# Seven slots for gathered rows where there were eight, three weight units kept and two parked, longer rows in two loads

## What is computed

```python
h = rmsnorm(x, norm_mix)
u_s5, x_lru, y_lru, g_a, g_b = split(h @ w_in)
a_out = s5_branch(u_s5, ...)          # diagonal complex scan, gelu, GLU (w_glu)
b_out = rglru_branch(x_lru, y_lru, ...)
merged = sigmoid(g_a) * (a_out @ w_proj_a) + sigmoid(g_b) * (b_out @ w_proj_b)
x = x + merged @ w_out
q = (rmsnorm(x, norm_ffn) @ w_q).reshape(C, 8, 2, 128)
s = einsum('chsk,hsnk->chsn', q, sub_keys)      # two top-16 lists, then top 16 of their sums
act = gelu(einsum('chkd,cd->chk', u_tab[eidx], x))
x = x + einsum('chk,chkd->cd', softmax(cs) * act, v_tab[eidx])
y = rmsnorm(x, norm_final)
```

## Time and profile before

| | before |
|---|---|
| median of three runs | 3239.21 us |
| the profiled execution | 3233.47 us, its span 3231.3 us |
| PE busy | 2726.6 us, 84% |
| DVE busy | 2491.7 us, 77% |
| ACT busy | 975.0 us, 30% |
| POOL busy | 1230.0 us, 38% |
| moved by DMA | 1245.43 MB, mean 385 GB/s |
| first gather | at 249.4 us |

### The profile page before, as it was taken

The page is one execution under the profiler, slowest core; times in us unless marked ns, Lnnn a source line. Parts: engine busy times, 40 slices in busy tenths (PEclk is TensorE's granted clock), DMA queues, the critical chain, the costliest instruction groups (busy, mean ns, idle before and its releaser), DMA issues.

```text
span 3231.3 us, 31776 instructions
## 1 busy us (share of the span) xinstructions
PE 2726.6 (84%) x9312; PEld 1564.3 (48%) x9312; DVE 2491.7 (77%) x5858; ACT 975.0 (30%) x3001; POOL 1230.0 (38%) x1048
## 2 busy tenths in 40 slices
PE   7988988999878989898879989899989895666566
PEld 6774544666444546555435545566534452222122
DVE  6836888888678898887669888887678887666754
ACT  2112433232134342322134432322133442222223
POOL 0003444344343443343344443333344343545553
PEclk9999999999989999999989999999999998787789
DMA  4269999999999999999999999999999998999997
GB/s 137 89 214 384 406 420 416 412 387 409 418 415 376 407 420 415 385 420 418 418 418 389 419 420 406 413 393 381 417 409 419 419 412 316 421 408 422 421 421 329
DMA packets 207197, 1245.43 MB, mean 385 GB/s; under 512 B 28056, under 2 KB 36632, under 8 KB 74928
## 3 DMA queue, kind: packets, MB, share of 16 engines
q0 software_dynamic: 148608, 1082.20, 81.6%
q1 hardware_dynamic: 56912, 156.36, 13.0%
q10 hardware_dynamic: 1504, 4.85, 0.4%
HBM read 1238.76 MB, written 4.55 MB: 385 GB/s over the span
## 4 chain that ended last, share of the span: by engine, by line
DMA 39%; PE 27%; DVE 23%; issue 3%; ACT 3%; DVEq 3%; POOL 2%; ACTq 1%; POOLq 0%
DMA arena<-in_uv,arena 39%; PE psum L1770 14%; DVE arena L1420 10%; PE psum L1671 7%; DVE arena L1020 4%; DVE arena L1012 3%; ACT arena L697 2%; PE psum L1815 2%; POOL arena L656 2%; PE psum L1686 1%; PE psum L1806 1%; PE psum L1827 1%; DVE arena L1261 1%; PE psum L1656 1%; PE psum L1706 1%
## 5 line engine op out<-in xcount | busy, mean ns | idle before, releaser
L656 POOL DMA_INDIRECT arena<-in_uv,arena x1032 | 1226.0, 1188 | 1973.8 <-PE psum L1770 1366.3
L1770 PE MATMUL psum<-arena 128*128 128x512 f32 x3192 | 1604.2, 647 | 434.8 <-ACT arena L697 400.5
L1420 DVE CUSTOM_DVE_ANT_0 arena<-arena 128x1024 f32<-128x1024 f32 x1024 | 1235.8, 1224 | 509.2 <-DMA arena<-in_uv,arena 478.2
L1770 PEld LDWEIGHTS psum<-arena 128*128 128x128 f32 x3192 | 621.6, 203 | 1264.7 <-issue 611.1
L697 ACT ACTIVATE arena<-arena 128x128 f32<-128x128 f32 (+3 forms) x2481 | 697.9, 313 | 1599.1 <-DVE arena L1420 1453.1
L1671 PE MATMUL psum<-arena 128*128 128x256 f32 (+1 forms) x2688 | 623.4, 387 | 12.3 <-DVE arena L1020 6.4
L1671 PEld LDWEIGHTS psum<-arena 128*128 128x128 f32 x2688 | 517.4, 194 | 142.9 <-issue 72.3
L1020 DVE SCALAR_TENSOR_TENSOR arena<-arena 128x1024 f32<-128x1024 f32 (+6 forms) x461 | 372.4, 814 | 64.3 <-ACT arena L697 34.2
L1012 DVE TENSOR_TENSOR arena<-arena 128x256 f32<-128x256 f32 (+10 forms) x832 | 284.9, 382 | 24.0 <-issue 1.6
L697 ACT ACTIVATE arena<-psum 128x256 f32<-128x256 f32 (+7 forms) x266 | 107.3, 414 | 574.9 <-PE psum L1671 506.4
L697 ACT ACT_TABLE_LOAD x113 | 145.0, 1283 | 4.0 <-PEq L2082 0.8
(11 more groups left out here) (99 smaller groups left out, 1020.8 us busy)
## 6 DMA issues: line engine op xcount, KB each, us to landing
arena<-in_w_in SPq DMA_DIRECT2D x112, 512.0 KB, 7.8
arena<-in_w_q SPq DMA_DIRECT2D x68, 512.0 KB, 11.2
arena<-in_w_ab SPq DMA_DIRECT2D x40, 512.0 KB, 7.8
arena<-in_w_out SPq DMA_DIRECT2D x40, 512.0 KB, 7.8
arena<-in_uv,arena POOLq DMA_INDIRECT x1032, 12.5
arena<-in_w_glu SPq DMA_DIRECT2D x16, 256.0 KB, 7.2
arena<-in_x_tok SPq DMA_DIRECT2D x8, 512.0 KB
arena<-in_keys SPq DMA_DIRECT2D x32, 128.0 KB, 7.4
```

What stands on the lines that cost most here:

```text
L656: pool.indirect_dma_start(uvring[:, r], None, i_["uv"], bass.IndirectOffsetOnAxis(column, 0)).then_inc(uv_in[r], 16)
L1420: V.tensor_tensor_reduce(out=u, in0=u, in1=hn[i // (SLOT // 2)], scale=1.0, scalar=0.0, op0=ALU.mult, op1=ALU.add, accum_out=dots_[:, b % ...
L1770: ins = mm(PV[:, half], dg[:, PAIR * (b % 2) + k], uvring[:, i % UV, at:at + 512], start=(i % (SLOT // 2) == 0), stop=(pe_slots(c, i + 1) ...
```

## The change

- `UV` goes from 8 to 7. The place of a gather in the ring is now its running number modulo 7 over the whole program, with the sample's eight gathers in the count (`place`, `sample_place`), and each gather waits for the one seven places before.
- `homes`: units `w_out` 2, `w_ab` 2 and `w_ab` 5 (`RESIDENT`) are loaded once in the program into places of their own; `w_out` 0 and 1 (`PARKED`) lie in `acc[1]` and `hn[1]` through chunk 0. Such a unit has no slot in the ring, and SP issues its one load without a wait. The ring counts only the others (`RINGED`, `ring_at`).
- `xT` is laid out on the host chunk by chunk, so that the load has one row of 8 KB (8.25 KB in the last chunk) in each partition.
- Keys come for two heads at once, 2 KB a partition, and lie in `gy`; before the first pair of a chunk SP waits for the end of the mix.
- To make room, `rstd` lies in `rT`, `ones` is one column read 128 times, `ztmp` lies in scratch, `pre` is gone, and `hS` is `s0`: the decay of the sample's states stands in `sample_states` behind the scans, in front of the GLU.

```diff
-UV = 8
+UV = 7
...
+RESIDENT = (("w_out", 2), ("w_ab", 2), ("w_ab", 5),)
+PARKED = (("w_out", 0), ("w_out", 1))
+HOMES = RESIDENT + PARKED
...
+def home(c, l):
+
+    kept = RESIDENT if c else HOMES
+    return HOMES.index(weight(c, l)) if weight(c, l) in kept else None
...
+RINGED = [[l for l in range(SLOTS if c else SLOTS0) if home(c, l) is None] for c in range(CH)]
...
+def place(c, i):
+
+    return SLOT * c + i + (HEADS if c == CH - 1 and i >= SA else 0)
...
+def sample_place(h):
+
+    return SLOT * (CH - 1) + SA + h
...
+        homes = [R.take(D) for _ in RESIDENT] + [acc[1], hn[1]]
...
             def load_weights(c, l):
 
-                g = slots(c) + l
-                w = weights[l] if c else weights0[l]
-                sp.dma_start(ring[:, g % RING, 0:w.shape[1]], w).then_inc(slot_in[g % RING], 16)
+                name, m = weight(c, l)
+                w = i_[name][m]
+                k = home(c, l)
+                if k is None:
+                    g = ring_at(c, l)
+                    sp.dma_start(ring[:, g % RING, 0:w.shape[1]], w).then_inc(slot_in[g % RING], 16)
+                elif c == 0 and WEIGHTS0.index((name, m)) == l:
+                    sp.dma_start(homes[k], w).then_inc(home_in[k], 16)
 
             def slot_free(c, l):
 
-                if l < RING:
-                    before, at = c - 1, (SLOTS if c > 1 else SLOTS0) - RING + l
-                else:
-                    before, at = c, l - RING
-                sp.wait_ge(unit, units(before) + slot_unit(at) + 1)
+                if home(c, l) is None:
+                    at = RINGED[c].index(l) - RING
+                    before = c if at >= 0 else c - 1
+                    sp.wait_ge(unit, units(before) + slot_unit(RINGED[before][at]) + 1)
...
-                sp.dma_start(hT[:, :, 0:n], i_["xT"][:, :, (c + 1) * C:(c + 1) * C + n]).then_inc(x_in, 16)
-
-            def keys(h, scores):
+                sp.dma_start(hT_all[:, 0:n], i_["xT"][:, at:at + n]).then_inc(x_in, 16)
+
+            def keys(pair, scores):
 
                 need(sp, s_mm, scores)
-                sp.dma_start(kb[:, h % 2], i_["keys"][:, 2 * h:2 * h + 2, :]).then_inc(key_in[h % 2], 16)
+                at = 4 * (pair % QT)
+                sp.dma_start(kb[:, pair % 2], i_["keys"][:, at:at + 4, :]).then_inc(key_in[pair % 2], 16)
...
-                    if l >= 48 and l % 2 == 0:
-                        h = (l - 48) // 2
-                        keys(h, lists(c) + h - 1)
+                    if l >= 48 and l % 4 == 0:
+                        pair = (l - 48) // 4
+                        if pair == 0:
+                            sp.wait_ge(unit, units(c) + U_OUT)
+                        keys(pair, lists(c) + 2 * (pair - 1))
...
-            def wait_free(c, i):
-
-                if on_dve(SLOT * c + i - UV):
-                    pool.wait_ge(v_dve, dve_slots(c, i - UV) + 1)
-                elif SLOT * c + i >= UV:
-                    pool.wait_ge(v_pe, pe_slots(c, i - UV) + 1)
+            def gather_to(at, column):
+
+                before = at - UV
+                if sample_place(0) <= before < sample_place(HEADS):
+                    pool.wait_ge(vs_pe, before - sample_place(0) + 1)
+                elif before >= 0:
+                    i = before - (HEADS if before >= sample_place(HEADS) else 0)
+                    if on_dve(i):
+                        pool.wait_ge(v_dve, dve_slots(0, i) + 1)
+                    else:
+                        pool.wait_ge(v_pe, pe_slots(0, i) + 1)
+                gather(at % UV, column)
...
             def slot(c, l):
-                g = slots(c) + l
+                k = home(c, l)
+                if k is not None:
+                    pe.wait_ge(home_in[k], 16)
+                    return homes[k]
+                g = ring_at(c, l)
                 pe.wait_ge(slot_in[g % RING], 16 * (g // RING + 1))
                 return ring[:, g % RING, :]
```

More of the change, by code:

```diff
@@ L67, with weight, ring_at @@
 SECOND_AT = 10
+TRUNK_W = [("w_in", m) for m in range(28)] + [("w_glu", m) for m in range(4)]
+MIX_W, OUT_W, QUERY_W = [[(name, m) for m in range(n)] for name, n in (("w_ab", 8), ("w_out", 8), ("w_q", 16))]
+WEIGHTS0 = TRUNK_W + MIX_W + OUT_W + MIX_W[0:4] + QUERY_W[0:2] + MIX_W[4:6] + QUERY_W[2:4] + MIX_W[6:8] + OUT_W \
+    + QUERY_W[4:16] + QUERY_W[0:4]
+WEIGHTS = TRUNK_W + MIX_W + OUT_W + QUERY_W
+RESIDENT = (("w_out", 2), ("w_ab", 2), ("w_ab", 5),)
+PARKED = (("w_out", 0), ("w_out", 1))
+HOMES = RESIDENT + PARKED
+def weight(c, l):
+    return WEIGHTS[l] if c else WEIGHTS0[l]
+def home(c, l):
+    kept = RESIDENT if c else HOMES
+    return HOMES.index(weight(c, l)) if weight(c, l) in kept else None
+RINGED = [[l for l in range(SLOTS if c else SLOTS0) if home(c, l) is None] for c in range(CH)]
+def ring_at(c, l):
+    return sum(len(RINGED[k]) for k in range(c)) + RINGED[c].index(l)
 TRUNK_DVE = "SSSSCSCSCSCSSSSSSS" + "LS" * 8 + "SS"
@@ L309, in build @@
         s0 = T.take(2, SJ, NS)
-        hT = T.take(KT, N)
+        hT_all = T.take(KT * N)
+        hT = [hT_all[:, 0:KT * columns(c)].rearrange("p (a b) -> p a b", a=KT) for c in range(CH)]
         ga = T.take(KT, N)
@@ L342, in build @@
         a_re, a_im = T.take(SJ), T.take(SJ)
[L343 to L344 removed]
+        hS = s0
         carr = T.take(2, SJ)
@@ L374, in build @@
         W = Arena(arena, T.at)
+        ztmp = W.take(QT, 6)
         braw = W.take(2, SJ, 16)
@@ L439, in build @@
         slot_in = [sem(f"slot_in{k}") for k in range(RING)]
+        home_in = [sem(f"home_in{k}") for k in range(len(HOMES))]
         key_in = [sem(f"key_in{k}") for k in range(2)]
@@ L574, in first_chunk @@
                     if l == 64:
-                        keys(2, 0)
-                        keys(3, 0)
+                        sp.wait_ge(unit, U_MIX1[KT - 1] + 1)
+                        keys(1, 0)
                     if l == 72:
                         next_columns(0)
-                    if l >= 72 and l % 2 == 0:
-                        h = (l - 64) // 2
-                        keys(h % HEADS, h - 1)
+                    if l >= 72 and l % 4 == 0:
+                        pair = (l - 64) // 4
+                        keys(pair, 2 * (pair - 1) if pair > 2 else 0)
                     slot_free(0, l)
@@ L674, in gathers @@
                         pool.wait_ge(s_mm, 2)
-                    wait_free(c, i)
-                    gather(i % UV, flat(idxn)[:, i:i + 1])
+                    gather_to(place(c, i), flat(idxn)[:, i:i + 1])
             for c in range(CH - 1):
@@ L684, in _ @@
             for h in range(HEADS):
[L685 to L691, removed]
+                gather_to(sample_place(h), iS[:, h:h + 1])
+            gathers(c, SA, SLOT)
         @block.scalar
@@ L1206, in c_tables, with sample_states, sample_conv @@
                 dve.sem_inc(s5_ok, 1)
[L1208 to L1216, removed]
+            def sample_states(c):
+                w = [flat(v)[:, 128 * k:128 * k + 128].rearrange("p (a b) -> p a b", b=NS) for v in (rc, rs) for k in range(2)]
+                dve.wait_ge(y_mm, SJ // 2 * (c + 1))
+                dve.wait_ge(smp_mm, 4)
+                for k, (a, x) in enumerate(((a_re, 0), (a_im, 1), (a_im, 0), (a_re, 1))):
+                    tt(w[k], over(a, NS), s0[:, x], ALU.mult)
+                dve.drain()
+                tt(s0[:, 0], w[0], w[1], ALU.subtract)
+                tt(s0[:, 1], w[2], w[3], ALU.add)
+                dve.drain()
+                tt(flat(hS.rearrange("p a b c -> p (a b) c")), flat(s0.rearrange("p a b c -> p (a b) c")),
+                   SB[0][:, 0:2 * SJ * NS], ALU.add)
+            def sample_conv():
                 for q in range(QT):
@@ L1416, in dots @@
                     i = PAIR * b + k
-                    again = 1 if c == CH - 1 and i >= SA else 0
-                    dve.wait_ge(uv_in[i % UV], 16 * (SLOT // UV * c + i // UV + 1 + again))
-                    u = uvring[:, i % UV, 0:D]
+                    at = place(c, i)
+                    dve.wait_ge(uv_in[at % UV], 16 * (at // UV + 1))
+                    u = uvring[:, at % UV, 0:D]
                     V.tensor_tensor_reduce(out=u, in0=u, in1=hn[i // (SLOT // 2)], scale=1.0, scalar=0.0, op0=ALU.mult,
@@ L1516, in first_lists @@
                 for m in range(5):
-                    mix(m, U_MIX1[m], late, MIXB[m % 2])
+                    mix(0, m, U_MIX1[m], late, MIXB[m % 2])
                 dve.wait_ge(s_ev, 1)
@@ L1593, in chunk @@
                     upto(at_mix(m) + 1)
-                    mix(m, units(c) + U_MIX + m, slice(0, n), MIXB[m % 2])
+                    mix(c, m, units(c) + U_MIX + m, slice(0, n), MIXB[m % 2])
                 upto(AT_X2)
```

77 lines of the change are left out of this document (35 added, 42 removed).

## The result

The changed kernel takes 3268.94 us (median of four runs, 3261.66 to 3273.88) where the kernel before takes 3239.03 (3235.65 to 3244.64): a ratio of 1.0092, 95% interval 1.008 to 1.0104. It is 30 us slower. The profiled execution has a span of 3271.8 us, 40.5 more than the one of before (3231.3): it is the slowest of its four, that of before the fastest. "Idle DMA time" of a stretch is its length times one less its DMA share.

What follows compares the result with a forecast made beforehand. The prediction took the DMA engines to set the pace after a start without gathers. A slot cost of 22.6 us less a gain of 17.8 gave +4.8 us, a median of 3244.0 us, range 3222 to 3272.

Steps and rivals of the forecast that it cites:

- rival 2: Stalls at nearly every trunk unit cost 52 us: +34, 3273 us; sign: idle DMA time up over 40 us; chance 0.21.
- The gain: Fewer weight loads, a shorter start and longer rows save 17.8 us in all, bounds 11.2 and 23.
- 12.0 + 2.0 + 1.0: us saved: nine loads in chunks 1 to 3, three w_out loads before the first gather, no w_out ring wait at start.
- 0.3 + 2.5: us saved: the first xT load at the start, then longer rows for later xT and key loads.
- The slot's cost: Seven slots instead of eight lose 22.6 us, where PE's trunk work frees no slot and queued gathers run out.
- Each of the seven grows by 2.49, 17.4 us: Seven existing DMA dips between 646 and 2722 us, idle 32.8 us, each lengthen by 2.49 us.
- The near misses: In 20 of 60 stretches of 50 us the fastest landing is below 7.9 us; shortfalls sum to 23.0, adjusted 22.6.
- In steady running nothing: Away from PE's trunk blocks, seven slots keep the DMA engines full in DVE's and PE's loops: 0 us lost.
- the 4 to 5 us to spare: DVE's loop spans 12.4 us and holds 8.3; PE's spans 17.4 and holds 12.7.
- 1 (elastic): Stalls move with late rows and weight loads fill near misses: loss 0 to 7 us, 3225 us; chance 0.20.
- 3 (freed DMA time isn't taken): PE lags in w_ab and w_out stretches, so nine fewer loads only add idle time: +17, 3256 us; chance 0.15.
- What to see: Signs: 1238.1 MB, fewer w_ab and w_out loads, landing median about 10 us, dips 2.5 us deeper, end unchanged, no w_out gap.

Runs made afterwards that it cites:

- d8_one: Changed kernel with eight slots, only w_out 2 kept and w_out 0 and 1 parked: 3231.87 us, 0.9967 of the kernel before.
- b7: Changed kernel, still seven slots, with no unit kept and none parked: 3281.73 us, 1.0137 of the kernel before.
- c8: Changed kernel with eight slots, no unit kept and none parked: 3233.73 us, 0.9976 of the kernel before.
- e6_keep: Changed kernel with six slots, the seventh place left empty: 3461.08 us, 1.0693 of the kernel before.
- a7: The changed kernel itself, run again as a control on another chip: 3269.53 us, 1.0084 of the kernel before.
- f7_split: Changed kernel with PE's blocks cut so a batch of values comes in between: 3253.29 us, 1.0049 of the kernel before.

## Why the prediction was right or wrong

**The frame** held: DMA-bound, with losses where slots aren't free in time. Forecast was +4.8 us, measured 29.9. The measured time is inside the range of 3222 to 3272 only because the range reaches to the rivals' times; the forecast's own range, -6 to +16, ends 14 us short of it. That the range held is luck, not a sign that the sum was right. The time is 4 us from rival 2 (3273).

**The gain**, 17.8 us, was right in size: 12.2 for the units with seven slots (12.0 + 2.0 + 1.0 expected for them) and 6.2 for the rest (0.3 + 2.5 expected). That the halves are 12.2 against 15.0 and 6.2 against 2.8, and only their sum fits, is luck in part, and 12.2 has an interval of 3 to 31. The start was 3.2 us shorter in the profiled execution, not 1.3, within the scatter told of above. Its two parts in the changed kernel, PE at the first w_out products and the chain's first load:

```profile
199.37 13.98 PE L1861 MATMUL psum<-arena 128*128 128x512 f32 x32 [0.99 <-issue]
```

```profile
0.75 4.86 DMA arena<-in_xT
```

The products run without the 0.97 us gap of the earlier trace rows, 32 instructions in one, and the load lands after 4.86 us against 5.7, 0.84 us where I took 0.3. They also start at 199.37 instead of 201.25, where I had said unchanged. Among the kernels with four weight slots they start between 199.4 and 202.0 (201.95 in d8_one, where the parked units give no gap either), so this can't be put down to a part of the change.

**The slot's cost** was the step that failed: 22.6 us expected, 48 measured. By its own terms:
- "Each of the seven grows by 2.49, 17.4 us": they grew by 9.6.
- The near misses: 22.6 less 17.4 left 5.2 us for them. I took the fastest landing of 50 us as the one near miss in it and its shortfall as the price. The idle time outside the seven dips grew by some 25 us, 6.5 of it at 374 alone. The price isn't bounded by one gather: a stall varies in length (3.72 or 5.41 us for the same sum), and places that weren't among the seven opened.
- The gathers' own time was put at nothing without a reason: q0 has 20 us more in the changed kernel and 12 more in b7 than in c8, for the same gathers.
- "In steady running nothing" came true (184 and 185 gathers in 475 us). But the 4 to 5 us to spare were too many: I had put together the fastest landing of all, 5.4 us, and the engines' times in one round of the last batches. In e6_keep the same loop's engines hold 8.65 us and not 7.3, at a granted clock of 0.70, and its landing 8.3. That this small spare is why new dips appeared is argued, not shown.

**The rivals.** 1 (elastic) is out by the cuts. 3 (freed DMA time isn't taken) is out as the whole story, since b7 is slower than a7, but it is at work: idle time rises by 7 to 12 us where units are kept, with eight slots as with seven. 2 has the size of the time. Of its mechanism the half is there: 18 places with idle time instead of 8, but not several in each 50 us, and the idle time grew by 35 us where its sign was over 40; the rest of the slot's price is in q0's longer time.

**What to see**: the end stage unchanged, the bytes, the counts of w_ab and w_out loads (32 and 34), and the w_out gap came as written. The seven dips deepened by 1.4 us each and not by 2.5, and the start of the w_out products moved. The median landing can't be read from the changed kernel's profile.

## What to carry to other kernels

A ring of buffers in front of a saturated DMA queue is worth what its longest consumer stall needs, and the price of a slot rises steeply as the ring gets short: here 192 us from six to seven, 48 from seven to eight, and perhaps 7 to 15 from eight to nine, an estimate. Weigh bytes saved (at most 1.3 us for 512 KB here, and less where the freed time stands idle) against that before memory moves from the ring to anything else. And cut the stall first: one batch let in between two PE blocks, at four places, gave 16 us with seven slots (11 by the ratios) at no cost in memory, about as much as the kept units did.

## What the runs showed of the hardware

The same 1032 gathers of the same 1082.20 MB kept the DMA engines busy for 2634 us with nine slots (q0's share times the span), 2637 to 2642 with eight, 2652 to 2662 with seven and 2742 with six. A packet's time is thus no constant: it is longer in the kernels with fewer slots. That packets issued into an empty queue take longer would fit, but f7_split, with less idle time than the changed kernel, has no shorter time on q0 (2662 against 2657); no run here separates it, and it stays open.

The length of its rows tells how fast a load lands beside gathers. The three later xT loads, 1 MB each, landed after 26.2 us in rows of 1 KB, and in rows of 8 KB, in the changed kernel, after 9.5 us in the median (9.8 in c8_nokeep, with the eight slots of before):

```profile
DMA to landing us min/median/max: 9.0/9.5/15.9
```

Nothing waits for them here, so this gave little.

The Trainium skill ("DMA: Bandwidth & Descriptors", Anatomy of one DMA) gives about 2.0 us + bytes / 436e3, an estimate of 4.4 us for such a gather. In e6_keep's loop 8.3 us pass from the end of the wait to the landing; that holds POOL's issue and what is left of two gathers issued before, so the page's figure is a floor for one gather alone and not what a loop should be reckoned with.
